# A decoder block's head: adaLN sums from VectorE to TensorE, hT in blocks of 128 rows, first pair reordered

## The reference, cut to what matters

```python
mod = jax.nn.silu(c) @ w_ada[layer] + b_ada[layer]              # c: (1, 1024), w_ada: (1024, 6144)
sh_a, sc_a, gt_a, sh_f, sc_f, gt_f = jnp.split(mod, N_MOD, axis=-1)
h = modulate(rms_norm(x, g_attn[layer]), sh_a, sc_a)            # h * (1 + scale) + shift
proj = h @ w_in[layer]                                          # w_in: (1024, 3072)
```

## Time and profile before

| | |
|---|---|
| median of 3 runs | 620.57 us (619.99 to 621.71) |
| the profiled execution | 618.37 us, span 616.4 us |
| TensorE busy | 543.3 us (88% of the span) |
| VectorE, ACT, GpSimd busy | 297.9, 184.3, 79.1 us |
| read from and written to HBM | 160.7 and 16.3 MB |

### The profile page before, as it was taken

One profiled execution on the slowest core, in us unless ns is written; L12 is line 12 of the kernel. 1 busy time (PEld: TensorE's weight loads), 2 busy tenths in 40 slices (PEclk: granted clock), 3 DMA queues, 4 the chain that ended last, 5 costly groups with the idle time before them and its releaser, 6 DMA issues.

```text
span 616.4 us, 7800 instructions
## 1 busy us (share of the span) xinstructions
PE 543.3 (88%) x3018; PEld 342.6 (56%) x3018; DVE 297.9 (48%) x523; ACT 184.3 (30%) x328; POOL 79.1 (13%) x101
## 2 busy tenths in 40 slices
PE   1689999999988999999999848899998999878797
PEld 1577768778766666665446524455544445434443
DVE  4988674366889736661032664233222223312216
ACT  5265562343454458872042211000000000000002
POOL 8132100000000000000041111112111111200000
PEclk9989999999999999999999869999999999999999
DMA  8987855495253074002920497999999999999957
GB/s 335 400 256 261 310 189 213 157 387 207 68 206 103 1 288 190 1 2 77 425 112 34 188 366 261 409 417 421 420 419 419 419 418 422 419 420 423 401 233 290
DMA packets 42626, 169.28 MB, mean 275 GB/s; under 512 B 7848, under 2 KB 9896, under 8 KB 30308
## 3 DMA queue, kind: packets, MB, share of 16 engines
q1 hardware_dynamic: 32356, 140.81, 57.3%
q0 software_dynamic: 9104, 25.95, 11.9%
q10 hardware_dynamic: 1136, 2.11, 0.9%
HBM read 160.74 MB, written 16.25 MB: 287 GB/s over the span
## 4 chain that ended last, share of the span: by engine, by line
PE 62%; DMA 13%; DVE 9%; SPq 8%; ACT 4%; issue 2%; DVEq 0%; POOLq 0%; ACTq 0%
PE banks L1833 11%; PE banks L1712 9%; PE banks L1853 5%; DMA qkT<-in_w_dram 5%; DMA obuf<-in_w_dram 4%; PE banks L1547 4%; PE banks L1549 4%; PE banks L1548 4%; PE banks L1664 3%; DMA stage<-in_w_in_dram 3%; PE banks L1648 2%; PE banks L1541 2%; PE banks L1539 2%; PE banks L1540 2%; SPq L455 2%
## 5 line engine op out<-in xcount | busy, mean ns | idle before, releaser
L859 ACT ACTIVATE work<-banks 128x256 f32<-128x256 f32 x16 | 6.1, 384 | 198.4 <-PE banks L1833 198.4
L1853 PE MATMUL banks<-stage,work 128*64 128x512 f32 x168 | 58.3, 598 | 6.3 <-ACT work L861 6.3
L1833 PE MATMUL banks<-qkT,work 128*64 128x256 f32 x272 | 61.5, 381 | 0.3 <-DMA stage<-in_w_dram 0.3
L1712 PE MATMUL banks<-stage,mixT 128*128 128x512 f32 x128 | 56.2, 594 | 0.0
L1356 DVE TENSOR_TENSOR work<-banks,gates 128x1024 f32<-128x1024 f32 x15 | 18.4, 1225 | 72.7 <-PE banks L1853 72.7
L1350 DVE TENSOR_TENSOR work<-work,banks 128x256 f32<-128x256 f32 x16 | 6.7, 422 | 87.4 <-ACT work L859 87.4
L1833 PE MATMUL banks<-hT,work 128*64 128x256 f32 x192 | 43.2, 381 | 2.8 <-DMA qkT<-in_w_dram 2.8
L1549 PE MATMUL banks<-hT_hi,w_lo 128*128 128x512 f32 x112 | 43.8, 391 | 0.0
L899 DVE SCALAR_TENSOR_TENSOR mixT<-stage,small,mixT 128x1024 f32<-128x1024 f32 x32 | 41.0, 1282 | 0.6
L1547 PE MATMUL banks<-hT_hi,w_hi 128*128 128x512 f32 x96 | 40.4, 421 | 0.0
L1712 PEld LDWEIGHTS banks<-stage,mixT 128*128 128x128 f32 x128 | 24.0, 190 | 28.9 <-issue 28.9
(11 more groups left out here) (304 smaller groups left out, 1156.4 us busy)
## 6 DMA issues: line engine op xcount, KB each, us to landing
stage<-in_w_dram SPq DMA_DIRECT2D x31, 1024.0 KB, 20.3
qkT<-in_w_dram SPq DMA_DIRECT2D x23, 1024.0 KB, 23.8
stage<-in_w_ada_dram POOLq DMA_DIRECT2D x16, 1024.0 KB, 5.7
hT<-in_w_dram SPq DMA_DIRECT2D x12, 1024.0 KB
stage<-in_w_in_dram SPq DMA_DIRECT2D x5, 2048.0 KB, 11.2
val<-in_w_dram SPq DMA_DIRECT2D x10, 1024.0 KB
mixT<-in_w_dram SPq DMA_DIRECT2D x10, 1024.0 KB
alibi<-in_w_dram SPq DMA_DIRECT2D x5, 1024.0 KB
```

Source lines behind the costliest of these rows:

```text
L1712: ins = mm(banks[:, w % 5, :], mixT[:, k, t * P:(t + 1) * P], wv[:, k % 4, half * 512:(half + 1) * 512], start=(k == 0), stop=(k == KD - 1))
L1833: ins = mm(banks[half * C:(half + 1) * C, 2, up * F:(up + 1) * F], heT[:, r, k * P + half * C:k * P + (half + 1) * C], ws[2 * place + half ...
L1853: ins = mm(banks[half * C:(half + 1) * C, 4 + 2 * r + col, :], geT[:, fc * P + half * C:fc * P + (half + 1) * C], w2s[2 * place + half][:, ...
```

## The change

Three things. (1) The input dimension is split among blocks differently: hT's block k holds rows 128k to 128k + 127 of h, so a turn reads contiguous columns, and w_in and the two bias vectors are read with the same split. (2) The shift and scale vectors are no longer summed on VectorE. TensorE multiplies each raw 128x128 tile of the weights with the column of cs of its row, and adds up the eight rows in PSUM, on top of the bias and g_attn rows that a small product has turned into columns. The last x tile is loaded between scale quarters 1 and 2. (3) ACT rounds chunk 1 after hT in place of before; VectorE makes hT_lo 0 among the hT_hi; the first pair runs chunk 1 with w_hi, then with w_lo, and takes the hT_lo in the order 0, 6, 7, 1 to 5.

```diff
-HEAD_FILLERS = ((KD // 2, 16), (KD - 1, 12))
+HEAD_FILLERS = (8, 14)
...
+        mod_rows = by_col[0:3 * KD, 0, 0:P]
...
-        in_v = w_in.rearrange("l (p k) n -> (l p) k n", k=KD)
+        in_v = w_in.rearrange("l (k p) n -> (l p) k n", p=P)
...
+        b_rows_v = b_ada.rearrange("l (v k p) -> (l v k) p", v=6, p=P)
...
             for i in range(4):
+                if i == 2:
+                    x_tile(NT - 1)
                 ada_quarter(scale_w, SCALE_A, i)
-            x_tile(NT - 1)
...
-            act.dma_start(b_col[:, 0:2, :], b_cols_v[:, SHIFT_A:SCALE_A + 1, :]).then_inc(mod_params_in, 16)
-            act.dma_start(g_col[:, 0, :], g_attn.rearrange("l (p k) -> (l p) k", k=KD)).then_inc(mod_params_in, 16)
+            act.dma_start(mod_rows[0:2 * KD, :], b_rows_v[SHIFT_A * KD:(SCALE_A + 1) * KD, :]).then_inc(mod_params_in, 16)
+            act.dma_start(mod_rows[2 * KD:3 * KD, :], g_attn.rearrange("l (k p) -> (l k) p", p=P)).then_inc(mod_params_in, 16)
...
             w_round(0)
-            w_round(1)
             act.wait_ge(mod_a, 1)
             for k in range(KD):
                 act.wait_ge(xT_done, k + 1)
                 a.activation(hT[:, k, :], banks[:, XT_BANK[k], :], ACT.Identity,
                              bias=mod[:, 0, k:k + 1], scale=mod[:, 1, k:k + 1]).then_inc(hT_raw, 1)
+            w_round(1)
             w_round(2)
...
-            first_sums(0, shift_w, shift_used)
-            first_sums(1, scale_w, scale_used)
...
-            w_rest(0)
-            dve.wait_ge(mod_params_in, 32)
-            dve.wait_ge(col_a, 1)
-            v.tensor_tensor(mod[:, 0, :], banks[:, 0, 0:8], b_col[:, 0, :], ALU.add)
-            link(v.tensor_tensor(mod[:, 1, :], banks[:, 0, 8:16], b_col[:, 1, :], ALU.add))
-            v.scalar_tensor_tensor(out=mod[:, 1, :], in0=mod[:, 1, :], scalar=1.0, in1=g_col[:, 0, :],
+            dve.wait_ge(shift_used, KD)
+            dve.wait_ge(scale_used, KD)
+            link(v.tensor_copy(mod[:, 0:2, :].rearrange("p v k -> p (v k)"), banks[:, 0, 0:2 * KD]))
+            v.scalar_tensor_tensor(out=mod[:, 1, :], in0=mod[:, 1, :], scalar=1.0, in1=banks[:, 0, 2 * KD:3 * KD],
                                    op0=ALU.add, op1=ALU.mult).then_inc(mod_a, 1)
             dve.wait_ge(mod_a, 1)
-            w_rest(1)
+            w_rest(0)
+            def hT_rest(k):
+                dve.wait_ge(hT_hi_ready, k + 1)
+                v.tensor_tensor(hT_lo[:, k, :], hT[:, k, :], hT_hi[:, k, :].bitcast(F32),
+                                ALU.subtract).then_inc(hT_lo_dve, 1)
             for k in range(KD):
                 dve.wait_ge(hT_raw, k + 1)
                 v.tensor_copy(hT_hi[:, k, :], hT[:, k, :]).then_inc(hT_hi_ready, 1)
-            for k in range(6):
-                dve.wait_ge(hT_hi_ready, k + 1)
-                v.tensor_tensor(hT_lo[:, k, :], hT[:, k, :], hT_hi[:, k, :].bitcast(F32),
-                                ALU.subtract).then_inc(hT_lo_dve, 1)
+                if k == KD // 2:
+                    hT_rest(0)
+            w_rest(1)
+            for k in range(1, 6):
+                hT_rest(k)
...
+            def column_quarter(v, i):
+                w, used = ((shift_w, shift_used), (scale_w, scale_used))[v]
+                pe.wait_ge(first_in[4 * v + i], 16)
+                for r in range(2 * i, 2 * i + 2):
+                    for k in range(KD):
+                        ins = mm(banks[:, 0, 8 * v + k:8 * v + k + 1], w[r // 4][:, r % 4, k * P:(k + 1) * P],
+                                 cs[:, r:r + 1], start=False, stop=(r == KD - 1), skip_group_check=True)
+                    ins.then_inc(used, 1)
+
+            pe.wait_ge(mod_params_in, 32)
+            mm(banks[:, 0, 0:3 * KD], mod_rows, ident[0:3 * KD, 0:3 * KD], start=True, stop=False, skip_group_check=True)
+            pe.wait_ge(silu_c, 1)
+            for i in range(4):
+                column_quarter(0, i)
+                if i < NT - 1:
+                    x_tile_T(i)
+            for i in range(3):
+                column_quarter(1, i)
+            x_tile_T(NT - 1)
+            head_fill(HEAD_FILLERS[0])
+            column_quarter(1, 3)
+            pe.wait_ge(mod_a, 1)
+            head_fill(HEAD_FILLERS[1])
             pe.wait_ge(hT_raw, 1)
             for t in range(NT):
                 ins = x_T(t, KD - 1)
...
+                pe.wait_ge(w_split, 1)
+                for k in range(KD):
+                    pe.wait_ge(hT_hi_ready, k + 1)
+                    mm(banks[:, 0, :], w_hi[:, k, 0:P], hT_hi[:, k, :], start=(k == 0), stop=False)
+                    mm(banks[:, 0, :], lo[:, k, 0:P], hT_hi[:, k, :], start=False, stop=False)
+                pe.wait_ge(w_hi_ready, 2)
+                for k in range(KD):
+                    mm(banks[:, 1, :], w_hi[:, k, P:2 * P], hT_hi[:, k, :], start=(k == 0), stop=False)
+                pe.wait_ge(w_split, 2)
+                for k in range(KD):
+                    mm(banks[:, 1, :], lo[:, k, P:2 * P], hT_hi[:, k, :], start=False, stop=False)
                 for c in range(2):
-                    for k in range(KD):
+                    for k in (0, 6, 7, 1, 2, 3, 4, 5):
```

More of the change, by code:

```diff
@@ L243, in hymba_block @@
         c_col, cs = cols(8), cols(8)
-        b_col = cols(32).rearrange("p (v k) -> p v k", v=4)
-        g_col = cols(16).rearrange("p (v k) -> p v k", v=2)
+        b_col = cols(16).rearrange("p (v k) -> p v k", v=2)
+        g_col = cols(8)
         mod = cols(32).rearrange("p (v k) -> p v k", v=4)
@@ L273, in hymba_block @@
         silu_c, shift_used, ada_used = sem("silu_c"), sem("shift_used"), sem("ada_used")
-        col_a, mod_a = sem("col_a"), sem("mod_a")
+        mod_a = sem("mod_a")
         xn_ready, xT_done = sem("xn_ready"), sem("xT_done")
@@ L351, in hymba_block @@
         params = [
-            (b_col[:, 2:4, :], b_cols_v[:, SHIFT_F:SCALE_F + 1, :]),
-            (g_col[:, 1, :], g_ffn.rearrange("l (p k) -> (l p) k", k=KD)),
+            (b_col, b_cols_v[:, SHIFT_F:SCALE_F + 1, :]),
+            (g_col, g_ffn.rearrange("l (p k) -> (l p) k", k=KD)),
             (out_g[:, 0:1], diff_out_g.rearrange("l (p o) -> (l p) o", o=1)),
@@ L907, in last_by_col @@
                                               in1=turned(sums), op0=ALU.mult, op1=ALU.add)
-            def first_sums(v, w, used):
-                for k in range(KD):
[L912 to L918, removed]
             v.memset(eps, EPS).then_inc(eps_ready, 1)
@@ L1005, in job_evac @@
                     w = job[1]
-                    v.tensor_tensor(mod[:, w, :], src[:, 0:8], b_col[:, w, :], ALU.add).then_inc(bank_free[n % 2], 1)
+                    v.tensor_tensor(mod[:, w, :], src[:, 0:8], b_col[:, w - 2, :], ALU.add).then_inc(bank_free[n % 2], 1)
                     dve.wait_ge(bank_free[n % 2], freed[job][1])
@@ L1009, in job_evac @@
                         link(v.scalar_tensor_tensor(out=mod[:, 3, :], in0=mod[:, 3, :], scalar=1.0,
-                                                    in1=g_col[:, 1, :], op0=ALU.add, op1=ALU.mult))
+                                                    in1=g_col, op0=ALU.add, op1=ALU.mult))
                         dve.wait_ge(wr_ready, 2)
@@ L1460, in x_T, with x_tile_T @@
                 return nc.tensor.transpose(banks[:, XT_BANK[k], t * P:(t + 1) * P],
[L1461 to L1480, removed]
+                                           xn[:, t, k * P:(k + 1) * P], ident)
+            def x_tile_T(t):
                 pe.wait_ge(xn_ready, t + 1)
@@ L1485, in _, with head_fill @@
                         ins.then_inc(xT_done, 1)
+            def head_fill(count):
+                for n in range(count):
+                    mm(banks[:, 0, 256:512], ones_bf[:], ones_bf[:].unsqueeze(1).to_broadcast([P, 2, P]),
+                       start=False, stop=True, skip_group_check=True)
+            def column_quarter(v, i):
[20 more added lines that the diff above has]
+            head_fill(HEAD_FILLERS[1])
             pe.wait_ge(hT_raw, 1)
@@ L1554, in first_pair @@
                 lo = w_lo_parts[:, 0, :].rearrange("p (k n) -> p k n", k=KD)
-                for c in range(2):
[L1556 to L1563, removed]
+                pe.wait_ge(w_split, 1)
[9 more added lines that the diff above has]
+                    mm(banks[:, 1, :], lo[:, k, P:2 * P], hT_hi[:, k, :], start=False, stop=False)
+                for c in range(2):
+                    for k in (0, 6, 7, 1, 2, 3, 4, 5):
                         if k < 6:
@@ L1568, in first_pair @@
                         ins = mm(banks[:, c, :], w_hi[:, k, c * P:(c + 1) * P], hT_lo[:, k, :], start=False,
-                                 stop=(k == KD - 1))
+                                 stop=(k == 5))
                     ins.then_inc(job_done, 1)
```

## The result

The changed kernel takes 654.58 us (median of 4 runs, 653.96 to 656.31) against 620.28 for the kernel before (median of 4, one more than in the table of before): 1.0563 times as long, 95% interval 1.0538 to 1.0589. 655 was forecast. The profiled execution took 654.63, its span is 652.7.

A forecast was written before the change was run, and what follows sets the result against it. The prediction took TensorE's 128 one-column products at 1.2 GHz to bound the changed head: hT's start +33.6 us, first pair +0.6, sum +34.2 on 618.37 profiled gives 652.6; with 2.2 for the median, 655, range 638 to 661.

The forecast's parts named there:

- The clock of the products: Head, TensorE: 128 one-column products all run at 1.2 GHz, 0.446 us each, 57.1 us; likeliest case, chance 0.76.
- The rule for weight loads: Head products: two weight loads cost 0.213 us at either clock, 27 us for all; the forecast did not adopt it.
- The bias and gain rows: Head, ACT's queue: the small loads land before 6.29 and cost nothing; other end 9.2, or +2.9 us.
- From hT's start to the end of the pair: End of head: 15.2 us against 14.6 before, so +0.6, with -1.1 and +3 as ends.
- One for one to the end: Behind the first pair: what the head loses after 35.72 is lost at the end, one for one.
- Nothing from the freed engines: Head, 6 to 35 us: VectorE's freed time has no user, since its next inputs come from mod; no gain.
- Rival 2: Head products run at 2.4 GHz after the first few us, or cost the same at either clock: 627.5 us, chance 0.10.
- Rival 3: Head: tile transposes or the 8 fillers raise the clock for part of the products, 638 to 648 us, chance 0.08.
- Rival 4: Head: raw tiles load in one pass, 0.115 us a product, TensorE follows DMA: 617.8 us, chance 0.04.

The follow-up runs named there:

- the run with 20 fillers: Changed kernel plus 24 unread 256-column bf16 products before the first product and 20 behind each row of eight but the last; 658.86 us, single execution.
- the two faster heads: Changed kernel with sums back on VectorE in contiguous order (619.18 us), and changed kernel with raw weights moving, cs column stationary (618.91 us).
- the run with 8 fillers: Changed kernel plus 24 unread 256-column bf16 products at the start and 8 behind each row but the last; 670.37 us (theory 641, its rival 668).

## Why the prediction was right, point by point

- **The clock of the products (128 at 1.2 GHz).** Right, and the step that carried the forecast. The chain has 53.9 us for them; with four tiles (6.4) and fillers (1.7) that is 62.0, where 57.1 + 7.0 + 1.8 - 3.4 = 62.5 was written. That the price goes with the clock is shown by the two runs with fillers (a row at 3.40 with the clock at 0.50, at 1.84 with 20 fillers a row). That narrow work left the clock low is shown by what changed when wide work came in: with 20 fillers a row all 16 rows, and with the operands swapped every quarter behind the first, ran at the higher level.
- **The rule for weight loads.** The Trainium skill ("TensorE: Matmul & The Clock Gate", section "LDWEIGHTS (loading the stationary operand)") has a load take its number of columns over 1.2, in ns, and says nothing of the clock; an estimate from that is 0.213 us for the two loads of a product. By the starts of neighbouring groups the trace agrees at 2.4 GHz (0.214, from 13.66 to 15.37 for eight) and doesn't at 1.2 (0.414, 6.62/16 in the chain). The measurement decides: for these products the price nearly doubles with the clock's fall.
- **The bias and gain rows.** Taken as landing before 6.29; they landed at 6.42 (1.74 + 4.68), later than the first quarter, and with the turn of 0.59 us the first product began at 7.14. Mis-sized by 0.85 us, which the sum of the products, 0.5 too large, partly took back. The first hT came at 69.64; 69.3 was written.
- **From hT's start to the end of the pair.** 15.1 us measured, 15.2 forecast. Of the two sums it was TensorE's (15.0) that ended the pair: it ran on without a gap from its fillers at 69.67 to 84.74. VectorE had its last hT_lo at 82.4, some 0.3 us ahead of the product that needs it, so the two were nearly level. The chance of up to 3 us more at a low clock didn't come; products were 0.23 us apart from 73.8 on.
- **One for one to the end.** Nearly. The head lost 84.74 - 50.32 = 34.4 us, the medians differ by 34.3. The profiled spans differ by 36.3; between the first and the last product with the experts' w2 the lag of the changed kernel grew from 34.6 (415.2 against 380.6) to 36.2 us (637.5 against 601.3), and in the last experts the profiled execution after had ten microseconds (614.5 to 624.5) at a mean clock of 0.83.
- **Nothing from the freed engines.** Right: VectorE idle for 67.5 us, DMA at 0.02 of its share ahead of hT.
- **Two readings of the rows of before were off, without effect on the sum.** The path to hT left out VectorE's w_lo of chunk 0, which stood ahead of the mod vectors until 35.25. And the issue of w_in's second piece at 40.09 was not released by the scale sums (32.68): SyncE's queue was issuing the small parameters up to 40.05. In the changed kernel the sums do hold it, to 69.13.
- **Rival 2 (2.4 GHz)** did not happen. Its price was right: in the run with 20 fillers a product costs what it said. **Rival 3 (in part)** didn't either: the last quarter, behind the 8 fillers, took 6.83 us like the others. **Rival 4 (a cheaper product)** is refuted by the same rows, with raw weights as stationary at 0.230. Its bound on the gain, ACT's rounding of chunk 0 at 34.0, held within 0.6 us in both kernels that do get there: 33.4, since their first piece of w_in came somewhat earlier too.

What stays open: how much of the head's 2.05 us the two faster heads keep. The medians say 0.4 and 0.7 with intervals of 0.8 us to either side; the places where the profiled executions gave it back are shown, each in one execution, but not how often a kernel meets them. Part 1, the split by 128 rows, never ran alone. And that it is the narrowness of the products that leaves the clock low, and not another property of them, rests on the comparison of forms; no run changed the width alone.

## What to carry to other kernels

For a matrix-vector product try the matrix moving and the vector stationary: the same raw f32 quarter cost TensorE 1.91 us that way and 6.83 us as 16 products of one column, which need two weight loads each (32 records a quarter) and were left at the lower clock. Ask as well what the move can win: here the limit of the head lay at 33.4 us for either engine. Before work moves to an engine that looks idle, multiply the number of instructions by the duration of that form *at the clock the place will have*, and look for a row of that form at both levels. When an experiment's total agrees with a theory, look whether its rows do: the run with 8 fillers met the wrong theory's time within 2.4 us.

## What the runs showed of the hardware

- TensorE busy all the time is no protection of its clock: from 30 to 50 us in the run with 8 fillers it was busy for all 20 us and granted 0.50.
- The granted clock column showed 1.00 in the first stretches of the kernels before and after while known forms ran at half speed (0.221 us a filler against 0.123, 3.57 us a burst against 1.95). In the runs with early fillers it says 1.00 from 3.6 to 6.0 us too, with 12 fillers in 2.4 us, 0.2 us each; from 11.5 us on, behind the first recorded fall, column and durations agree.
- Products into different groups of 32 output partitions ran side by side: eight records of 512 moving f32 columns in 1.91 us, 0.24 each, where records into all 128 partitions start 0.43 us apart (16 in 7.11 us in the output projection before).
- Stretches far behind the head lost the clock in some profiled executions and not in others: 1.7 us ahead of the experts with the sums on VectorE, 1.3 in the experts with swapped operands, 1.6 there in the changed kernel, nearly as much as the 2.05 us that the best head won. Whether the shift of the head decides it isn't shown, each being one execution.
- An hT_lo of 512 columns took VectorE 0.68 us alone and 1.77 to 1.79 beside GpSimd's.
